# The first router moved into the output projection of the first mixer, and first loads of stages issued one stage ahead

## The reference

```
xs = x_sample + position                                  # latent rows only
hs = modulate(rmsnorm(xs, g), shift1, scale1)
ms = hyena_mixer(hs)                                      # in-projection, short conv, long conv, times gate, @ out_w
xs = xs + gate1 * ms
h  = modulate(rmsnorm(xs, g2), shift2, scale2)
aff = softmax(h @ w_router)                               # 16 affinities a token
gate, idx = top_k(aff over tokens, cap)                   # cap = 128 latent, 16 context slots of each expert
xs = xs + gate2 * scatter_add(idx, gate * swiglu_expert(h[idx]))
```

## Time and profile before

| | |
|---|---|
| median of 3 runs | 4111.65 us (4111.37 to 4113.6) |
| the profiled execution | 4110.46 us, of which span 4108.8 us |
| PE busy | 3548.7 us (86% of the span) |
| DVE busy | 1824.8 us (44%) |
| ACT busy | 1283.2 us (31%) |
| mean granted TensorE clock | 0.912 of full |
| `phase_front` | 0 to 111 us |
| `phase_hyena_in` | 111 to 478 us |
| `phase_long_conv` | 478 to 921.5 us |
| `phase_hyena_out` | 921.5 to 1049.9 us |
| `phase_route`, layer 0 | 1049.9 to 1160.3 us, of which the choice of slots from 1120.4 us |
| `phase_norm` and start of `phase_ssd_in` | 1952.1 and 1996.4 us |

### The profile page before, as it was taken

One profiled execution on the slowest core, in us unless ns is written; L12 is line 12 of the kernel. 1 busy time (PEld: TensorE's weight loads), 2 busy tenths in 40 slices (PEclk: granted clock), 3 DMA queues, 4 the chain that ended last, 5 costly groups with the idle time before them and its releaser, 6 DMA issues. The chain is left out here.

```text
span 4108.8 us, 58638 instructions
## 1 busy us (share of the span) xinstructions
PE 3548.7 (86%) x23807; PEld 2966.2 (72%) x23807; DVE 1824.8 (44%) x2981; ACT 1283.2 (31%) x2027; POOL 436.6 (11%) x410
## 2 busy tenths in 40 slices
PE   4899888888669999998699997759997499999995
PEld 2899634336559999997599997425554489999994
DVE  5333354544443333333501554768886633333332
ACT  3222301101313332232412433226564322323332
POOL 0000000000011112111000110510000012211111
PEclk7999798898579999999799998879999599999997
DMA  7466302016647878884321222886764568878885
GB/s 214 151 204 214 119 8 69 0 50 216 246 152 273 298 278 297 297 293 145 115 93 59 88 93 69 314 320 221 229 230 147 218 219 297 295 280 290 287 288 176
DMA packets 383661, 806.61 MB, mean 196 GB/s; under 512 B 21351, under 2 KB 65884, under 8 KB 382091
## 3 DMA queue, kind: packets, MB, share of 16 engines
q1 hardware_dynamic: 348892, 711.90, 49.0%
q0 software_dynamic: 28400, 86.70, 7.6%
q10 hardware_dynamic: 6240, 6.29, 0.5%
HBM read 695.92 MB, written 108.90 MB: 196 GB/s over the span
## 5 line engine op out<-in xcount | busy, mean ns | idle before, releaser
L1737 PEld LDWEIGHTS moe_banks<-moe_xt,mix_ring 128*128 128x128 f32 x8192 | 1011.7, 191 | 5.5 <-issue 3.2
L1737 PE MATMUL moe_banks<-moe_xt,mix_ring 128*128 128x144 f32 x8192 | 1013.0, 287 | 3.1 <-ACT moe_xt L1772 3.1
L62 PE MATMUL ssdin_banks<-h_leading,ssdin_w_split 128*128 128x384 f32 x1920 | 385.5, 334 | 5.8 <-ACT ssdin_pad L2033 2.9
L1759 PE MATMUL moe_banks<-moe_down_parts,moe_hid_parts 128*128 128x512 f32 x1536 | 357.6, 392 | 0.0
L62 PEld LDWEIGHTS ssdin_banks<-h_leading,ssdin_w_split 128*128 128x128 f32 x1920 | 337.1, 188 | 7.2 <-issue 7.2
L1759 PEld LDWEIGHTS moe_banks<-moe_down_parts,moe_hid_parts 128*128 128x128 f32 x1536 | 285.9, 188 | 71.4 <-issue 13.2
L1817 DVE TENSOR_TENSOR moe_hid<-moe_banks,moe_sg 128x128 f32<-128x128 f32 x256 | 74.6, 292 | 581.5 <-ACT moe_sg L1795 581.5
L1807 DVE TENSOR_TENSOR moe_down_parts<-mix_ring,moe_down_parts 128x2048 fp32r<-128x2048 f32 x128 | 292.2, 2283 | 0.0
L1704 POOL DMA_INDIRECT x_dram<-moe_yc,mix_idx_quarter x128 | 167.3, 1307 | 1088.5 <-DVE moe_yc L1828 1059.2
L2585 PE MATMUL scan_banks<-scan_w,scan_yc 128*128 128x512 f32 x576 | 256.0, 598 | 0.0
L62 PE MATMUL hyin_banks<-h_leading,hyin_w_split 128*128 128x384 f32 x1152 | 237.6, 337 | 11.5 <-DVE hyin_w_split L742 11.5
(11 more groups left out here) (355 smaller groups left out, 4531.0 us busy)
## 6 DMA issues: line engine op xcount, KB each, us to landing
mix_ring<-in_moe_w_gate SPq DMA_DIRECT2D x64, 2048.0 KB, 7.9
mix_ring<-in_moe_w_up SPq DMA_DIRECT2D x64, 2048.0 KB, 12.9
mix_ring<-in_moe_w_down SPq DMA_DIRECT2D x64, 2048.0 KB, 17.4
early_ada<-in_ada_w SPq DMA_DIRECT2D x96, 512.0 KB, 5.7
scan_cum<-row_dram SPq DMA_DIRECT2D x36, 1024.0 KB, 6.1
ssdin_w<-in_ssd_in_w SPq DMA_DIRECT2D x10, 2048.0 KB, 9.6
scan_states<-s_dram SPq DMA_DIRECT2D x36, 512.0 KB, 7.8
s_dram<-st_state SPq DMA_DIRECT2D x16, 1024.0 KB, 9.4
```

The costliest lines, as they stand in the source:

```text
L62: ins = pe.matmul(out(piece), w_at(w[a], k), h_k(h[b], k, piece), start=(k == 0 and a == 0 and b == 0), stop=(k == KD - 1 and a == 1))
L1737: ins = pe.matmul(pb[:, 2 * (f % 2) + j, 0:SLOTS], ring[:, 2 * half + j, k, col:col + P], xt[:, k, :], start=(k == 0), stop=(k == KD - 1))
L1759: ins = pe.matmul(pb[:, LAT_BANK[half], :], hid_parts[:, a, k, :], wd[:, half, b, k, :], start=(k == 0 and a + b == 0), stop=(k == KD - 1 ...
```

## The change

The per-tile work of the first router goes into the loop of the output projection as a class `Router`; the choice of slots becomes a class `Choice`, used in layer 1's `phase_route` as before and in a small stage `phase_choose` of layer 0, which also issues the first expert's weight loads. g is read through a ring of three tiles in place of one large tile. First loads are issued in the stage before: conv_first in `phase_hyena_in`, out_w in the last half of `phase_long_conv`, ssd_first in `phase_norm`. In `phase_front` the filter's three columns become rows of the parameter stage (turned on PE with the others), ssd_D is loaded as one row to all partitions and copied twice by DVE, ada_b moves from POOL's to ACT's queue, the filter's loads go ahead of ada_w, and PE turns the parameters and does the filter's first layer before piece 0. Tiles of several stages share one area (`hyena_work`). Layer 1's router works as before.

```diff
@@ phase_front @@
             def _(sp):
                 ...
+                filt.load(sp)
                 mod.load(sp, 0)
-                filt.load(sp)
                 for n in range(1, FRONT_PIECES):
                     mod.load(sp, n)
             def _(pool):
+                for n, name in enumerate(("hy_f_b1", "hy_f_b2", "hy_f_freq")):
+                    for half in range(2):
+                        pool.dma_start(stage[F_ROW + n:F_ROW + n + 1, 3, half * HY_HID:(half + 1) * HY_HID], io[name]
+                                       ).then_inc(s_stage, 16)
                 for n, (source, at, cnt) in enumerate(keep["param_rows"]):
                     pool.dma_start(stage[at[1]:at[1] + cnt, at[0], :], source).then_inc(s_stage, 16)
-                for h in range(2):
-                    pool.dma_start(keep["d_skip"][h * HEAD:(h + 1) * HEAD, :],
-                                   bass.AP(io["ssd_D"].tensor, h, [[0, HEAD], [2, Z_TILES]]), ...)
-                ... (4 loads of ada_b)
+                pool.dma_start(d_all[:, :], io["ssd_D"].partition_broadcast(P)).then_inc(s_d, 16)
             def _(act):
                 ...
+                ... (the 4 loads of ada_b, behind the two Silu)
                 filt.sine(act, 0)
             def _(pe):
-                pe.wait_ge(s_silu, 2)
-                mod.product(pe, 0, pb[:, PIECE_BANK[0], 0:P])
-                filt.products(pe, pb, 0)
-                pe.wait_ge(s_stage, 16 * (len(keep["param_rows"]) + 2))
+                pe.wait_ge(s_stage, 16 * (len(keep["param_rows"]) + 6))
                 for n, cnt in enumerate(keep["param_counts"]):
                     pe.transpose(...)
+                pe.wait_ge(s_silu, 2)
+                filt.products(pe, pb, 0)
+                mod.product(pe, 0, pb[:, PIECE_BANK[0], 0:P])
                 mod.product(pe, 1, pb[:, PIECE_BANK[1], 0:P])
                 filt.products(pe, pb, 1)
@@ Filter.load @@
-            for n, name in enumerate(("hy_f_b1", "hy_f_b2", "hy_f_freq")):
-                eng.dma_start(self.col[at, n:n + 1], io[name].rearrange("a h -> h a")).then_inc(s_in, 16)
@@ phase_hyena_in, end of SP's list @@
+                mod.finished(sp, 23)
+                conv_first(sp, io, keep)            # negt and filter half 0
@@ phase_long_conv, SP, behind the loads of x0 @@
+                    if h:
+                        for half in range(2):
+                            sp.dma_start(keep["hyout_w"][:, :, cols], io["hy_out_w"]...).then_inc(keep["s_hyout_w"][half], 16)
@@ phase_hyena_out @@
 SP      +  load_g(0), load_g(1), gate, load_x(0), load_g(2), load_x(1), router.load(sp), load_x(2),
 SP      +  then for t in range(3, TILES): load_g(t); load_x(t)
 ACT     +                lead(1)
         +                for t in range(TILES + 3):
         +                    if t < TILES:
         +                        act.wait_ge(s_sum, t + 1)
         +                        router.stats(act, t, xr[:, t % 3, :])
         +                    if t + 2 < TILES:
         +                        lead(t + 2)
         +                    if 1 <= t <= TILES:
         +                        router.keep_turned(act, t - 1)
         +                    if 2 <= t <= TILES + 1:
         +                        router.exps(act, t - 2)
 PE      +                for t in range(TILES + 3):
         +                    if t < TILES:
         +                        project(t, 0)
         +                    if 2 <= t <= TILES + 1:
         +                        router.logits(pe, t - 2)
         +                    if t >= 3:
         +                        router.turn_affinities(pe, t - 3)
         +                    if t < TILES:
         +                        project(t, 1)
         +                    if 1 <= t <= TILES:
         +                        router.turn(pe, t - 1)
 DVE     +                for t in range(TILES + 3):
         +                    if t < TILES:
         +                        residual(t)
         +                    if 2 <= t <= TILES + 1:
         +                        router.top(dve, t - 2)
         +                    if t + 2 < TILES:
         +                        rest(t + 2)
         +                    if t < TILES:
         +                        router.rows(dve, ch, t, xr[:, t % 3, :])
         +                    position(t + 2)
         +                    if 2 <= t <= TILES + 1:
         +                        router.soft(dve, ch, t - 2)
         +                    if t >= 3:
         +                        router.keep_affinities(dve, t - 3)
@@ class Router, the waits that tie the engines @@
+    def logits(self, pe, t):
+        pe.wait_ge(self.s_ht, t + 1)
+        if t:
+            pe.wait_ge(self.s_ex, t)                # one bank: exp of tile t - 1 is through
+    def turn_affinities(self, pe, t):
+        pe.wait_ge(self.s_af, t + 1)                # softmax of tile t by DVE
+    def keep_turned(self, act, t):
+        act.wait_ge(self.s_tr, t + 1)
+    def exps(self, act, t):
+        act.wait_ge(self.s_mx, t + 1)
+    def rows(self, dve, ch, t, x):
+        dve.wait_ge(self.s_rt, t + 1)
@@ phase_choose @@
+            def _(sp):
+                for j in range(PIECES):
+                    sp.dma_start(keep["ring"][:, j, :, :], expert_piece(io, layer, j, 0)).then_inc(keep["s_ring"][j], 16)
+            def _(pe):
+                choice.turn(pe)
+            def _(dve):
+                choice.choose(dve, ch)
+                choice.tables(dve)
@@ phase_norm (layer 1), end of SP's list @@
+                ssd_first(sp, io, keep)             # wdt, the two columns, pieces 0 and 1 of in_w
@@ mixture @@
-        phase_route(nc, io, keep, layer)
+        if layer:
+            phase_route(nc, io, keep, layer)
+        else:
+            phase_choose(nc, io, keep, layer)
@@ build: three more scopes (hyena_, early_, ssd_), each with its own clearing and barrier at its end @@
```

More of the change, by code:

```diff
@@ L120 @@
 FRONT_PIECES = 4
+F_ROW = 16
 COND_PAD = 32
@@ L291, in _ @@
                 for c in range(2):
-                    act.activation(cond_t[:, :, c], pb[:, 7, 8 * c:8 * c + 8], ACT.Silu).then_inc(s_silu, 1)
+                    act.activation(cond_t[:, :, c], pb[:, 0, 8 * c:8 * c + 8], ACT.Silu).then_inc(s_silu, 1)
+                act.wait_ge(s_rows0, 1)
+                for layer in range(2):
+                    for c in range(2):
+                        act.dma_start(rows[c::32, layer * 12:layer * 12 + 12, :], row_blocks(io["ada_b"][layer])
+                                      ).then_inc(s_bias, 16)
                 filt.sine(act, 0)
@@ L1120, in _ @@
                     for tt in (0, 16):
-                        step(tt_(taps[0:1, tt, :], taps[0:1, tt, :], fbias[:, :], ALU.add))
+                        step(tt_(taps[0:1, tt, :], taps[0:1, tt, :], fbias, ALU.add))
                     done()
@@ L1259, in phase_hyena_out @@
         pb = m.psum()
+        router = Router(m, io, keep, 0, pb, 4, 6, 7)
         s_pos = [m.sem(f"pos_in{b}") for b in range(2)]
         s_xp = m.sem("position_added")
[L1262 to L1263 removed]
+        s_g = [m.sem(f"g_in{b}") for b in range(G_RING)]
+        s_w = keep["s_hyout_w"]
         s_gate = m.sem("gate_in")
@@ L1294, in _ @@
                         sp.dma_start(pos[:, t % 2, :], io["pos"][(t - 1) * P:t * P, :]).then_inc(s_pos[t % 2], 16)
+                load_g(0)
+                load_g(1)
+                for c in range(2):
+                    sp.dma_start(gate[:, c, :], io["vec_dram"][0, c, V_G1:V_G1 + 1, :].partition_broadcast(P)).then_inc(s_gate, 16)
+                load_x(0)
+                load_g(2)
+                load_x(1)
+                router.load(sp)
+                load_x(2)
+                for t in range(3, TILES):
+                    load_g(t)
+                    load_x(t)
             @block.scalar
@@ L1344, in _ @@
+                for t in range(TILES + 3):
+                    if t < TILES:
+                        project(t, 0)
+                    if 2 <= t <= TILES + 1:
+                        router.logits(pe, t - 2)
+                    if t >= 3:
+                        router.turn_affinities(pe, t - 3)
+                    if t < TILES:
+                        project(t, 1)
+                    if 1 <= t <= TILES:
+                        router.turn(pe, t - 1)
             @block.vector
             def _(dve):
+                ch = Chain(dve, router.s_dve)
@@ L1376, in _ @@
                     dve.tensor_tensor(xr[:, t % 3, :], xr[:, t % 3, :], t1[:, t % 2, :], ALU.add).then_inc(s_sum, 1)
+                rest_of_weights(0)
+                rest(0)
+                rest_of_weights(1)
+                rest(1)
+                ch.link(dve.memset(keep["cur"][:, 0, :], -1.0))
+                dve.wait_ge(s_gate, 32)
+                position(1)
+                for t in range(TILES + 3):
+                    if t < TILES:
+                        residual(t)
```

(15 more changed lines are left out.)

468 lines of the change are left out of this document (310 added, 158 removed).

## The result

The kernel after takes 4071.6 us (median of four, 4067.0 to 4073.7) against 4112.6 of the kernel before in the same comparison: a ratio of 0.9899, 95% interval 0.9881 to 0.9916, 41 us less. The forecast was 29.3 less. The profiled executions differ by 36.9 in their spans, 4108.8 and 4071.9; the other four lie in which run was profiled (before's is 2 us under its median, after's 2 over).

What follows compares the result with a forecast made beforehand. Projection bound by PE, router by small transposes and 16-column products, choice by DVE, stage heads by loads they issue. 13.2 + 6.7 + 6.1 + 4.6 - 1.3 = 29.3 us less: median 4082, range 4057 to 4098.

Steps and rivals of the forecast that it cites:

- Step 1: First stage: filter columns no longer hold SP 10.9 us and delay PE's filter products and ada_w pieces; minus 13.2 us.
- Steps 2, 3 and 5: Heads of long convolution, output projection, SSD input projection: loads issued earlier; minus 6.7, 10.4 (inside Step 4's term) and 4.6 us.
- Step 4: Output projection merged with router: period 20.2 us a tile, bounds 17.6 and 22.8; choice starts 6.1 us earlier.
- the ring: Merged stage: PE, ACT and DVE wait on each other in turn, period 17.6 us at full clock, not PE's own 14.0.
- the two waits: Merged stage: each period PE's logits wait for ACT's exp (9.1 us), its affinities for DVE's softmax (11.8 us).
- the clock: Merged stage: PE's clock falls to half after its waits, taking the period from 17.6 to 20.2 us.
- a low spell each period: Merged stage: half clock each period, losing 2.1 us in the second half's matmuls and 0.5 in the logits.
- Step 6: Three more scopes, at 0.4 us each: plus 1.3 us.
- The rule weighed: ACT's table loads in the merged stage: the skill page's 1380 ns drain per switch would add 10 us, 4092; chance 0.03.
- The clock holds: Rival, merged stage: full clock despite waits, period 17.6 us, 51.5 us less in all, 4060; chance 0.24.
- The small loads are late: Rival, first stage: POOL's six more loads delay PE, gain 5 in place of 13.2 us, 4090; chance 0.12.
- The clock stays low throughout: Rival called slower: half clock through the whole merged stage, period 26.4 us, total 4146; chance 0.03.

Runs made afterwards that it cites:

- front_columns: Kernel after, with the filter's three columns loaded by SP one number a partition, behind piece 0, and waited for as before: 4074.3 us, ratio 0.9910.
- before_d: Kernel before, with one edit: ssd_D loaded as one row to all partitions and copied twice by DVE: 4092.0 us, ratio 0.9959.
- own_loads: Kernel after, with first loads of long convolution, output projection and SSD input projection issued by those stages themselves again: 4096.0 us, ratio 0.9967.
- regroup: Kernel after, with both halves of a tile's projection done before the logits, affinities and transposes of earlier tiles: 4034.2 us, ratio 0.9816.
- filler: Kernel after, with 12 unused 512-column matmuls in each of tiles 3 to 8, between the projection's first half and the logits: 4063.0 us, ratio 0.9884.
- best: The kernel regroup, with PE also multiplying piece 0 of ada_w while the small loads are under way: 4031.9 us, ratio 0.9819.

## Why the prediction was right, and where it wasn't

- **Step 1, the first stage.** Right in sign, its reason wrong. The forecast took SP's 10.9 us in two loads of columns, and PE's wait for them, as the cost of the columns. Both were effects: front_columns has the same loads in a stage of 94.2 us, and before_d has them in one of 92.5. The step that failed is that the old form of ssd_D's load was put at nothing without a reason: the forecast names ssd_D only in its new form, as "issued by 10, used after 29", which asks what it costs its user and not what it does to the others. The row that would have told it was in the list of DMA issues of before: 4 KB, 19.5 us to landing. The 13.2 came near by luck: the columns were what PE waited for, whatever held them, and the change happened to take away what held them. With ssd_D gathered as before and every other edit kept (spread) the stage is 105.5, only 4.9 under before. The 4.1 between 49.0 and 44.9 are the small loads (1.0), pieces 1 and 3 in 7.9 and 7.7 in place of 8.9, and the second layer at full clock, 2.6 for 4.1, less 0.6 in piece 2; in the other six profiles piece 3 ended at 45.0 to 47.2.
- **Steps 2, 3 and 5, the heads.** Right, to 0.2 us: 6.5 for 6.7, 10.5 for 10.4, 4.7 for 4.6. own_loads shows them one by one. What it showed beyond: where a head is late, what comes behind it on the same queue is late too.
- **Step 4, the merged stage.** Right in its mechanism: the ring, the two waits, the clock. Taken from the stage's start, the forecast had PE's first product at 9.4, tile 1's end at 33.7, and tiles 4 to 7 in 80.8 us; it was 9.3, 33.3 and 80.9. The choice came 185.4 us into the stage and not 192.8; the 7.4 lie at the ends of the loop. Tile 2 took 14.0 and not 16.8 (its logits are the first and wait for no exp), tile 3 took 17.9 and tile 8 17.2, where a low spell was in the forecast but the trace has half of one. The terms that were mis-sized are "a low spell each period", for tiles 3 and 8, and for tile 2 the wait as well as the spell.
- **Step 6, scopes.** 0.5 to 0.6 each, for 0.4.
- **The rule weighed.** In the ring the root follows its table load by 0.01 us (988.45 plus 1.28, then 989.74), and exp likewise; nor is there a pause ahead of the load, which starts 0.02 us behind the copy before it (990.89 plus 1.00, then 991.91). The drain of about 1380 ns that the Trainium skill (ScalarE: Activation LUTs, What ACT_TABLE_LOAD costs) adds to each switch is not in this case's traces; with it exp, and the logits behind it, would have come 1.4 later.
- **The rivals.** "The clock holds" is what regroup made true, and filler in four of six tiles, and not this kernel. "The small loads are late" did not come: 14.7 for 15.7. "The clock stays low throughout" neither: in 80.9 us of the merged stage it was 0.83 on the mean. The first expert waited for its gathered rows and ACT, not for weights.

Where did the gain of the largest edit go? Into a new wait. Merging took the router's 70 us away and put 6 to 9 us on most tiles of the projection (10.9 before), of which only 2.7 are PE's work; the rest is the ring (17.8 for 13.6) and its clock (2.4). Its tail at half clock, some 21 us, is new too.

## What to carry to other kernels

When work of several engines is merged into a loop, place each short product where its operand has been ready for some time, behind the long products of the round and not between them: the same instructions in another order were worth 37 us here, the merging in its first order 3. And before a wait is charged to the load it names, look at what the DMA engines did meanwhile: a window with a high DMA share and few GB/s has its cause in another load, and the list of issues with their time to landing names it.

## What was new about the hardware

- Two loads of 4 KB that gather 4-byte elements held the DMA engines almost alone for 20 us. In the records of single packets they are 32 packets of 256 bytes, 8.4 us each at the median, from 10.9 to 31.3 us, as many as two for each of the 16 engines; 64 elements in 8.4 us are 0.13 us an element. Packets of 256 bytes of SP's queue took 0.018 us at the median in the same first 35 us. Six loads of the columns with 64 numbers of 4 bytes each, on SP's queue, cost nothing of the kind. Why these are so much cheaper (the queue, the pattern, or the number of elements, 384 for 2048) was not tried.
- In tiles 4 to 7 the clock went to half for 6.8 us in each period, beginning 0.8 to 1.7 us after PE had resumed from a wait of 2.7 us, and back to full without a change in what PE did. In the tail of regroup and of best it fell some 3.6 us into a wait of 5.4.
- Matmuls that nobody reads bought time twice: with 12 of them a tile took 17.8 in place of 20.2 (two tiles of the four in the middle; the other two took 20.7 and 19.4), and the tail 16.5 in place of 20.8.
